# Projections and gates as high and low parts: gate chunks ahead of modulation chunks, x loaded first, attention's low parts on VectorE between the softmax steps

## The chip, the cores and the metric

One core of one Trainium2 chip. The metric is the device time of one launch in microseconds (us), lower is better. TensorE (PE), VectorE (DVE), ScalarE (ACT), GpSimd (POOL) and SyncE (SP, which issues the weight DMAs) each run a program of their own, in order, and meet at semaphores.

## The reference

Two layers of a four-branch mixer with an FFN over 256 tokens of width 1024, then a second block (a state-space scan, attention and experts), which the change doesn't touch. Of a layer:

```python
h = rms_norm(x, norm_mix_pre[l])
proj = h @ w_in[l]                                   # q, k, v, conv and pool inputs
... # compressed, selected, window and sink attention; conv; pooling
up = jnp.einsum("bsnc,ncd->bsnd", branches, w_branch[l])
gates = jax.nn.sigmoid((h @ w_gate[l]).reshape(bsz, seq, N_BRANCH, D_MODEL))
mix = jnp.einsum("bsnd,bsnd->bsd", gates, up) @ w_o[l]
x = x + rms_norm(mix, norm_mix_post[l])
hf = rms_norm(x, norm_ffn_pre[l])
u = causal_depthwise_conv(hf @ ffn_w_up[l], ffn_conv_w[l], ffn_conv_b[l])
gate, val = jnp.split(u, 2, axis=-1)
x = x + rms_norm((jax.nn.gelu(gate) * val) @ ffn_w_down[l], norm_ffn_post[l])
```

The second block also needs `silu(c) @ w_mod`, the modulation, which depends on no token.

## The kernel before

All matrices stream through one ring of four slots of 1 MB (128 x 2048 float32). SP reloads a slot when TensorE has given it back; a layer has 92 chunks, in the order in which TensorE takes them. TensorE gives a chunk back with the next product behind it (`release`, then `carry`), or with the chunk's own last one (`done_with`).

Products exist in two kinds. Plain float32 ones take a chunk straight from the ring: the projections kv, kv2, q and dq (L498, two chunks each, token-major, 512 columns), and the feature-major chunks c, ba, bg and gate (`blocks_fm`, L526, 16 products of 256 columns). The up, wo and FFN products use reduced-precision float32 (fp32r) three times in place of one: high x high, high x low and low x high. For these ACT rounds a chunk to its high part (`split_hi`, L386) and VectorE subtracts it from the chunk, which gives the low part (`split_lo`, L392).

The order of a layer is written out by hand for each engine. First four modulation chunks (`mods`, 0 and 1) run, then the transposition of the normed x (`ht`, L435), the projections, "ga" (the gates of the attention parts), c, ba, the compression (L555), bg. Then comes the attention loop. It has twelve items: for each half t of the queries three kinds of attention (selected, window, sink), each in two groups. An item has one block of 128 keys for t = 0 (the first six items) and two for t = 1. Pass i is, on TensorE: scores of item i (L640), a gate chunk, the transposition of item i-1's probabilities (`turn_probs`), its values (L666). On ACT: the gate's copy out, the copies of the transposed probabilities, the exponentials of item i. On VectorE: `mask(i)` (an add from PSUM, L1136, and a reduction, L1141 or L1144), `weigh(i-1)`, ten steps of the depthwise convolution (L1096). Two more gate chunks stand in passes 3 and 6, one in `cmp_out`, and behind the first eight gate chunks stands a modulation chunk each (`mod_half`, L448), with a turn (L467) every second time.

Behind the loop come the convolution's turn, the up products with the gates, wo, the residual and norm, the FFN.

Of the kernel before, what the change touches and what calls it, by code (L numbers as in the profile page):

```python
# [50 lines left out]
SPLITS = 3  # L51
FFN_CHUNKS = FB + FB // 2
# [5 lines left out]
def offsets(fields):  # L58
# [11 lines left out]
    ("w_ga", KD * 24),  # L70
])
ROWS, N_ROWS = offsets([("mix_post", D), ("ffn_post", D), ("sinks", 8)])
# [123 lines left out]
def plan_mods(jobs, steps):  # L196
    for i in steps:
        jobs.plan(("mod", i))
        if i - 1 in steps:
            jobs.plan(("modT", i - 1))  # L200


EARLY_MODS, MID_MODS = range(0, 2), range(2, MOD_STEPS)


def plan_layer(jobs):
    plan_mods(jobs, EARLY_MODS)
# [3 lines left out]
    jobs.plan(("modT", EARLY_MODS[-1]))  # L211
# [16 lines left out]
    for kv in range(2):  # L228
        jobs.plan(("hidT", kv), drains=2)
    jobs.plan(("bg", 1))  # L230
# [49 lines left out]
def layer_block(nc, l, mem, ring, landed, used, wts, psum, sems, cols_dram, rows_dram, loaded):  # L280
# [28 lines left out]
    lo_ready = sems("lo_ready")  # L309
# [9 lines left out]
    x, tm, hT, proj, gates, qTs, rkT = (mem[k] for k in ("x", "tm", "hT", "proj", "gates", "qTs", "rkT"))  # L319
# [3 lines left out]
    cdT = gates[:, 2048:3072].rearrange("p (m t) -> p m t", m=4)  # L323
    rtmp = gates[:, 3072:4480]
    rot = gates[:, 4480:7296].rearrange("p (t c) -> p t c", t=2)
    hfT, fT, split = (mem[k] for k in ("hfT", "fT", "split"))
# [9 lines left out]
    sg = sc[:, :, :, :].rearrange("p b j k -> p (b j k)")[:, 0:1024].rearrange("p (i c) -> p i c", i=2)  # L336
    pooled_in = mem["tmp"][:, :, :].rearrange("p i c -> p (i c)").rearrange("p (g t) -> p g t", g=4)
    small = mem["small"]
    mixT, bglu, cpad, acc, tmp, mixS, split2 = (mem[k] for k in ("hT", "bglu", "cpad", "acc", "tmp", "mixS", "split2"))
# [30 lines left out]
    n_up = 12  # L370
    first_ffn = N_LAYER_CHUNKS - 1 - FFN_CHUNKS
    first_up = first_ffn - n_up

    def split_slot(n):

        if n < n_up:
            return first_up + n, split2[:, n % 2, :, :], 2
        return first_ffn + n - n_up, split[:, (n - n_up) % SPLITS, :, :], SPLITS

    def split_hi(act, n):  # L380

        c, slot, turns = split_slot(n)
        if turns <= n < n_up or n >= n_up + turns:
            act.wait_ge(used[(c - turns) % SLOTS], l * (N_LAYER_CHUNKS // SLOTS) + ((c - turns) // SLOTS + 1))
# [3 lines left out]
    def split_lo(dve, n):  # L388

        c, slot, _ = split_slot(n)  # L390
        dve.wait_ge(hi_ready, n + 1)
        dve.tensor_tensor(slot[:, 1, :], ring[:, c % SLOTS, :], slot[:, 0, :].bitcast(F32), ALU.subtract).then_inc(lo_ready, 1)  # L392

    with nc.Block() as block:
# [11 lines left out]
        def _(pe):  # L406
# [49 lines left out]
            def mod(i):  # L456
                mod_half(i, 0)
                mod_half(i, 1)

            def mod_turn(i):  # L460

                jobs.wait_drained(pe, ("mod", i))
                if i == 0:
                    pe.wait_ge(loaded, 32)
# [8 lines left out]
            def mods(steps):  # L473
                for i in steps:
                    mod(i)
                    if i - 1 in steps:
                        mod_turn(i - 1)


            mods(EARLY_MODS)  # L480
            pe.wait_ge(loaded, 32)
# [4 lines left out]
            mod_turn(EARLY_MODS[-1])  # L486


            for w in ("kv", "kv2", "q", "dq"):
                for half in range(2):  # L490
                    chunk = next_chunk().rearrange("p (k n) -> p k n", k=4)
                    for t in range(TT):
                        if w == "kv":
                            jobs.wait_drained(pe, ("ht", half, t))
                        if half == 0:
                            jobs.claim(pe, (w, t))
                        for k in range(4):
                            mm = pe.matmul(jobs.out((w, t)), hT[:, 4 * half + k, t * P:(t + 1) * P], chunk[:, k, :],  # L498
                                           start=(half == 0 and k == 0), stop=(half == 1 and k == 3))
                            if k == 0:  # L500
                                carry(mm)
                        if half == 1 and t == 0:
# [9 lines left out]
            for t in range(TT):  # L512
                for k in range(KD):
                    mm = pe.matmul(jobs.out("ga")[:, 24 * t:24 * t + 24], hT[:, k, t * P:(t + 1) * P],
                                   C("w_ga", 24 * k, 24 * k + 24), start=(k == 0), stop=(k == KD - 1))
                    if k == 0:
                        carry(mm)
            jobs.fill(mm, "ga")

            def blocks_fm(name):  # L520

                chunk = next_chunk().rearrange("p (k m) -> p k m", k=KD)
                jobs.claim(pe, name)
                for b in range(2):
                    for k in range(KD):
                        mm = pe.matmul(jobs.out(name)[:, b * T:(b + 1) * T], chunk[:, k, b * P:(b + 1) * P], hT[:, k, :],  # L526
                                       start=(k == 0), stop=(k == KD - 1))
                        if k == 0:
                            carry(mm)
                jobs.fill(mm, name)  # L530
                return name

# [6 lines left out]
            for t in range(TT):  # L539
                jobs.wait_drained(pe, ("q", t))  # L540
                transpose4(("qT", t), [proj[:, t, 1024 + i * P:1024 + (i + 1) * P] for i in range(4)])
                pe.wait_ge(roped, 3 * t + 1)
# [21 lines left out]
            for kv in range(2):  # L564
# [7 lines left out]
                jobs.fill(mm, ("hidT", kv))  # L572
            release(blocks_fm(("bg", 1)))
# [15 lines left out]
            for t in range(TT):  # L589
                pe.wait_ge(roped, 3 * t + 2)  # L590
                transpose4(("rqT", t), [rot[:, t, 384 + i * P:384 + (i + 1) * P] for i in range(4)])
                pe.wait_ge(roped, 3 * t + 3)
# [96 lines left out]
            def next_split(n):  # L689

                c, slot, _ = split_slot(n)
                assert state["chunk"] == c, (state, c)
                state["chunk"] += 1
                pe.wait_ge(lo_ready, n + 1)
                return slot[:, 0, :], slot[:, 1, :]


            for bi, n in enumerate(BRANCH_ORDER):
                for half in range(2):
# [4 lines left out]
                    hi, lo = (part.rearrange("p (k n) -> p k n", k=4) for part in next_split(2 * bi + half))  # L704
# [20 lines left out]
            for c in range(2):  # L725
                for half in range(2):
                    hi, lo = (part.rearrange("p (k n) -> p k n", k=4) for part in next_split(8 + 2 * c + half))
# [24 lines left out]
            pe.wait_ge(h_lo, 2 * TT)  # L752
            for j in range(FB):
                hi, lo = (part.rearrange("p (k m) -> p k m", k=KD) for part in next_split(n_up + j))
# [14 lines left out]
            for i in range(FB // 2):  # L769
                hi, lo = (part.rearrange("p (k n) -> p k n", k=2) for part in next_split(n_up + FB + i))  # L770
# [20 lines left out]
            assert state["chunk"] == N_LAYER_CHUNKS, state  # L791
# [2057 lines left out]
```

## Time and profile before

| | |
|---|---|
| median of 3 runs | 2058.55 us (2053.18 to 2112.91) |
| the profiled execution's own time | 2053.64 us |
| its span | 2051.8 us |
| TensorE, VectorE, ACT, GpSimd busy | 91%, 46%, 32%, 11% |
| layer 0, layer 1, second block | about 0 to 645, 645 to 1265, 1265 to 2052 |

The profile shows one execution. A row of a timeline merges equal instructions that follow one another: it gives their start, the time they cover, their count and the idle time before them, with what ended it. A float32 product stands in it as two instructions. Where single products are listed, the difference of two starts is the pace, since the durations overlap.

### The profile page before, as it was taken

The numbers are of one execution on the slowest core, as the hardware profiler recorded it, in microseconds if no ns is written. First come the engines' busy times: TensorE is split into PE (matmuls) and PEld (weight loads), VectorE is DVE, ScalarE is ACT, GpSimd is POOL, SyncE is SP. The second block draws the span as 40 slices with busy tenths as digits, with TensorE's granted clock in tenths as the row PEclk, the third lists the DMA queues.
The fourth block names the chain that finished last, engine by engine and source line by source line (L and its number), as shares of the span: only waits on it lengthen the run. The fifth ranks groups of instructions, "written<-read, shape, count | busy, mean of one in ns | idle before, by whom it ended". The sixth has DMA issues, their size and how long they took to land. (4 is left out here: it accounts for less than half of the span.)

```text
span 2051.8 us, 24867 instructions
## 1 busy us (share of the span) xinstructions
PE 1860.6 (91%) x9940; PEld 1444.6 (70%) x9940; DVE 953.2 (46%) x1410; ACT 647.4 (32%) x987; POOL 217.5 (11%) x285
## 2 busy tenths in 40 slices
PE   6999998869996999998869997999899997899996
PEld 3577777869974477676859985544476645799995
DVE  1235464557742215454646743138434415355555
ACT  1122225445531112224545542111223401333331
POOL 0100000213310010000303320001520001000000
PEclk9999999989998999999989998899978997899998
DMA  7444422425455444522425545322110021355552
GB/s 275 143 185 164 185 84 102 152 106 182 180 182 219 163 184 145 204 85 80 154 97 182 185 168 188 123 82 82 41 42 1 1 103 62 106 183 189 179 183 82
DMA packets 39094, 279.81 MB, mean 136 GB/s; under 512 B 4432, under 2 KB 4688, under 8 KB 5840
## 3 DMA queue, kind: packets, MB, share of 16 engines
q1 hardware_dynamic: 37984, 272.44, 36.5%
q10 hardware_dynamic: 1008, 5.93, 0.8%
q8 instruction: 74, 1.21, 0.2%
q14 instruction: 28, 0.23, 0.0%
HBM read 277.30 MB, written 1.05 MB: 136 GB/s over the span
## 5 line engine op out<-in xcount | busy, mean ns | idle before, releaser
L526 PE MATMUL psum<-sb_hT,ring 128*128 128x256 f32 x1408 | 321.9, 388 | 2.2 <-DMA ring<-weights 2.1
L526 PEld LDWEIGHTS psum<-sb_hT,ring 128*128 128x128 f32 x1408 | 270.2, 194 | 49.1 <-issue 7.7
L392 DVE TENSOR_TENSOR sb_split<-ring,sb_split 128x2048 fp32r<-128x2048 f32 x90 | 212.4, 2360 | 123.7 <-ACT sb_split L386 123.4
L759 PE MATMUL psum<-sb_hfT,sb_split 128*128 128x256 f32 x704 | 201.4, 286 | 10.9 <-DVE sb_hfT L1279 10.9
L386 ACT ACTIVATE sb_split<-ring 128x2048 fp32r<-128x2048 f32 x90 | 171.9, 1910 | 114.9 <-PE psum L781 57.8
L762 PE MATMUL psum<-sb_hfT,sb_split 128*128 128x256 f32 x704 | 201.0, 286 | 0.0
L763 PE MATMUL psum<-sb_hfT,sb_split 128*128 128x256 f32 x704 | 200.9, 285 | 0.0
L1644 DVE TENSOR_TENSOR sb_split<-ring,sb_split 128x2048 fp32r<-128x2048 f32 x48 | 110.0, 2292 | 160.2 <-ACT sb_split L1639 160.2
L1937 PE MATMUL psum<-sb_hfS,sb_split 128*128 128x256 f32 x512 | 146.5, 286 | 2.5 <-PE psum L1959 2.1
L1940 PE MATMUL psum<-sb_hfS,sb_split 128*128 128x256 f32 x512 | 146.0, 285 | 0.0
L1941 PE MATMUL psum<-sb_hfS,sb_split 128*128 128x256 f32 x512 | 145.9, 285 | 0.0
L759 PEld LDWEIGHTS psum<-sb_hfT,sb_split 128*128 128x128 f32 x704 | 137.1, 195 | 11.4 <-DVE sb_hfT L1279 11.4
L762 PEld LDWEIGHTS psum<-sb_hfT,sb_split 128*128 128x128 f32 x704 | 137.1, 195 | 0.0
L763 PEld LDWEIGHTS psum<-sb_hfT,sb_split 128*128 128x128 f32 x704 | 137.0, 195 | 0.0
L1639 ACT ACTIVATE sb_split<-ring 128x2048 fp32r<-128x2048 f32 x48 | 91.6, 1908 | 95.8 <-PE psum L1898 47.0
L498 PE MATMUL psum<-ring,sb_hT 128*128 128x512 f32 x256 | 110.4, 593 | 0.0
L1937 PEld LDWEIGHTS psum<-sb_hfS,sb_split 128*128 128x128 f32 x512 | 99.4, 194 | 4.2 <-issue 3.8
L1309 DVE SCALAR_TENSOR_TENSOR sb_hq<-psum,sb_cols,sb_hq 128x254 f32<-128x254 f32 (+1 forms) x176 | 72.7, 475 | 61.8 <-ACT sb_hq L969 61.8
L1940 PEld LDWEIGHTS psum<-sb_hfS,sb_split 128*128 128x128 f32 x512 | 99.5, 194 | 0.3
L1941 PEld LDWEIGHTS psum<-sb_hfS,sb_split 128*128 128x128 f32 x512 | 99.4, 194 | 0.0
L1096 DVE SCALAR_TENSOR_TENSOR sb_acc<-sb_bglu,sb_cols,sb_acc 128x256 f32<-128x256 f32 x240 | 97.1, 476 | 0.0
L809 ACT ACTIVATE sb_gates<-psum 128x512 f32<-128x512 f32 x36 | 21.3, 597 | 232.7 <-PE psum L526 232.1
(352 smaller groups left out, 3221.2 us busy)
## 6 DMA issues: line engine op xcount, KB each, us to landing
ring<-weights SPq DMA_DIRECT2D x256, 1024.0 KB, 4.8
sb_rows<-rows ACTq DMA_DIRECT2D x2, 1028.0 KB, 10.6
sb_rows<-rows ACTq DMA_DIRECT2D x1, 2048.0 KB, 10.4
sb_cols<-cols ACTq DMA_DIRECT2D x2, 662.0 KB, 6.2
sb_x<-x_in SPq DMA_DIRECT2D x1, 1024.0 KB, 6.9
sb_y<-ctx_in SPq DMA_DIRECT2D x1, 1024.0 KB, 5.6
out<-sb_x SPq DMA_DIRECT2D x2, 512.0 KB, 2.7
sb_const<-const SPq DMA_DIRECT2D x1, 791.0 KB, 9.8
```

What stands on the lines that cost most here:

```text
L386: act.activation(slot[:, 0, :], ring[:, c % SLOTS, :], ACT.Copy).then_inc(hi_ready, 1)
L392: dve.tensor_tensor(slot[:, 1, :], ring[:, c % SLOTS, :], slot[:, 0, :].bitcast(F32), ALU.subtract).then_inc(lo_ready, 1)
L498: mm = pe.matmul(jobs.out((w, t)), hT[:, 4 * half + k, t * P:(t + 1) * P], chunk[:, k, :], start=(half == 0 and k == 0), stop=(half == 1 a ...
L526: mm = pe.matmul(jobs.out(name)[:, b * T:(b + 1) * T], chunk[:, k, b * P:(b + 1) * P], hT[:, k, :], start=(k == 0), stop=(k == KD - 1))
L759: mm = pe.matmul(out, hi[:, k, b * P:(b + 1) * P], hfT[:, 0, k, :], start=(k == 0), stop=False)
L762: pe.matmul(out, hi[:, k, b * P:(b + 1) * P], hfT[:, 1, k, :], start=False, stop=False)
L763: mm = pe.matmul(out, lo[:, k, b * P:(b + 1) * P], hfT[:, 0, k, :], start=False, stop=(k == KD - 1))
L1096: conv.up(dve.scalar_tensor_tensor(out=acc[:, b, :], in0=bglu[:, b, k:k + T], scalar=w, in1=acc[:, b, :], op0=ALU.mult, op1=ALU.add))
L1644: dve.tensor_tensor(split[:, n % SPLITS, 1, :], ring[:, (first_moe + n) % SLOTS, :], split[:, n % SPLITS, 0, :].bitcast(F32), ALU.subtract ...
L1937: mm = pe.matmul(out, hi[:, k, b * P:(b + 1) * P], hfS[:, 0, k, :], start=(k == 0), stop=False)
L1940: pe.matmul(out, hi[:, k, b * P:(b + 1) * P], hfS[:, 1, k, :], start=False, stop=False)
L1941: mm = pe.matmul(out, lo[:, k, b * P:(b + 1) * P], hfS[:, 0, k, :], start=False, stop=(k == KD - 1))
```

## The change

- c, ba, bg, gate and the four projections are done in three fp32r products. hS holds the high and low part of the normed, scaled x. High parts of chunks go to two shared buffers (hi; four in the FFN), low parts to a ring of their own, ring_low, with one slot per ring slot. In the attention loop VectorE takes the low part of gate chunk i+1 between `mask(i)` and `weigh(i-1)`, and ACT takes the high part of gate k+2 directly behind the copy of gate k.
- "ga" is computed with the weights held and 256 columns moving, and turned afterwards.
- The early modulation is gone: the six steps stand as twelve chunks behind gate chunks 0 to 11. Passes 3 and 6 have no second gate chunk; pass 12 has one. Gates are taken in the order of the branches.
- x and the constants are loaded ahead of the ring. The rows table is loaded behind the projections, its FFN part later still, into the same place.
- Buffers are laid out anew.

```diff
+def layer_chunks():
+    out = ["split"] * 12 + ["raw"] * 4 + ["split"] * 2
+    for i in range(16):
+        out.append("split")
+        if mid_mod_of(i) is not None:
+            out.append("raw")
+    return out + ["split"] * (12 + FFN_CHUNKS) + ["raw"]
...
+FIRST_C, FIRST_BA, FIRST_BG, FIRST_GATE, FIRST_UP, FIRST_WO, FIRST_FFN, FIRST_DOWN = 8, 10, 12, 14, 30, 38, 42, 64
...
     def split_hi(act, n):
+        before = n - HI_MIX if n <= FIRST_FFN else n - HI_FFN if n >= FIRST_FFN + HI_FFN - 1 else -1
+        if before >= 0:
+            c = SPLIT_CHUNKS[before]
+            act.wait_ge(used[c % SLOTS], l * (N_LAYER_CHUNKS // SLOTS) + (c // SLOTS + 1))
+        c = SPLIT_CHUNKS[n]
         act.wait_ge(landed[c % SLOTS], (l * (N_LAYER_CHUNKS // SLOTS) + (c // SLOTS + 1)) * 16)
-        act.activation(slot[:, 0, :], ring[:, c % SLOTS, :], ACT.Copy).then_inc(hi_ready, 1)
+        act.activation(hi_of(n), ring[:, c % SLOTS, :], ACT.Copy).then_inc(hi_ready, 1)
...
             def blocks_fm(name):
-                chunk = next_chunk().rearrange("p (k m) -> p k m", k=KD)
+                hi, lo = (part.rearrange("p (k m) -> p k m", k=KD) for part in next_split())
...
-                        mm = pe.matmul(jobs.out(name)[:, b * T:(b + 1) * T], chunk[:, k, b * P:(b + 1) * P], hT[:, k, :],
-                                       start=(k == 0), stop=(k == KD - 1))
+                        mm = pe.matmul(out, hi[:, k, bs], hS[:, 0, k, :], start=(k == 0), stop=False)
...
+                        pe.matmul(out, hi[:, k, bs], hS[:, 1, k, :], start=False, stop=False)
+                        mm = pe.matmul(out, lo[:, k, bs], hS[:, 0, k, :], start=False, stop=(k == KD - 1))
...
                     scores(i)
-                gate_chunks(i < len(ITEMS))
+                gate_chunks(1)
                 if i == 1:
                     cmp_out()
                 if i >= 1:
                     turn_probs(i - 1)
-                    gate_chunks(i in (3, 6))
                     values(i - 1)
...
                     i = gate_at["n"]
                     if i < 16:
-                        copy_out(("gate", i), gates[:, i * 512:(i + 1) * 512])
+                        n = BRANCH_ORDER[i // 4]
+                        copy_out(("gate", i), gate_of[n][:, i % 4 * 512:(i % 4 + 1) * 512], func=ACT.Sigmoid if n == BRANCH_ORDER[-1] and i > 13 else ACT.Copy)
+                        split_hi(act, FIRST_GATE + i + 2)
...
+            gate_lows = iter(range(FIRST_GATE, FIRST_GATE + 13))
+            split_lo(dve, next(gate_lows))
             for i in range(len(ITEMS) + 1):
                 if i < len(ITEMS):
                     mask(i)
+                    split_lo(dve, next(gate_lows))
...
+            split_lo(dve, FIRST_GATE + 13)
             out_low(len(ITEMS) - 1)
-            split_lo(dve, 0)
             conv_steps(4 * TAPS)
+            for n in range(FIRST_GATE + 14, FIRST_UP + 1):
+                split_lo(dve, n)
...
                     sp.dma_start(mem["cond"][:, :], cond).then_inc(conditioned, 16)
+                    sp.dma_start(mem["x"][:, :, :], x_in.rearrange("(t p) d -> p t d", p=P)).then_inc(loaded, 16)
+                    sp.dma_start(mem["const"][:, :], const).then_inc(placed, 16)
                     for s in range(SLOTS):
                         sp.dma_start(ring[:, s, :], weights[s]).then_inc(landed[s], 16)
```

ACT in the attention loop, one pass of before (pass 2): the gate's copy out, the modulation's, the transposed probabilities', the exponentials.

```order
L809 ACTIVATE sb_gates<-psum 128x512 [waits filled_a1]
L809 ACTIVATE sb_mrow<-psum 128x512 [waits filled_a3]
L809 ACTIVATE sb_pt<-psum 128x512 [waits filled_t]
L873 ACTIVATE sb_sc,sb_small<-sb_sc,sb_small 128x128 [waits masked]
L873 ACTIVATE sb_sc,sb_small<-sb_sc,sb_small 128x128 x3
```

The same place in the changed kernel. The chunk of the high part is in slot 0 (landed_0), and so was the gate chunk whose copy stands first; ISA is a wait for that slot's release.

```order
L822 ACTIVATE sb_tm<-psum 128x512 [waits filled_a2]
L403 ISA [waits used_0]
L404 ACTIVATE sb_hi<-ring 128x2048 [waits landed_0]
L822 ACTIVATE sb_mrow<-psum 128x512 [waits filled_a0]
L822 ACTIVATE sb_pt<-psum 128x512 [waits filled_t]
L906 ACTIVATE sb_sc,sb_small<-sb_sc,sb_small 128x128 [waits masked]
L906 ACTIVATE sb_sc,sb_small<-sb_sc,sb_small 128x128 x3
```

The high part has come between the gate's copy and the copy of the probabilities.

VectorE in the same loop, pass 3 of before: mask, weigh, convolution.

```order
L1136 TENSOR_TENSOR sb_sc<-psum,sb_const 128x4x128 [waits filled_s,filled_t]
L1141 TENSOR_REDUCE sb_small<-sb_sc 128x4 [waits drained_s]
L1164 RECIPROCAL sb_small<-sb_small 128x4 [waits exped]
L1167 TENSOR_TENSOR sb_small<-sb_small 128x4 [waits v_order]
L1170 TENSOR_TENSOR sb_sc<-sb_sc,sb_small 128x4x128 [waits v_order]
L1096 SCALAR_TENSOR_TENSOR sb_acc<-sb_bglu,sb_cols,sb_acc 128x256 [waits conv_done] x10
```

VectorE in pass 3 of the changed kernel (filled_s is the scores' signal).

```order
L1197 TENSOR_TENSOR sb_sc<-psum,sb_const 128x4x128 [waits filled_s,filled_t]
L1202 TENSOR_REDUCE sb_small<-sb_sc 128x4 [waits drained_s]
L410 TENSOR_TENSOR ring_low<-ring,sb_hi 128x2048 [waits hi_ready]
L1226 RECIPROCAL sb_small<-sb_small 128x4 [waits exped]
L1229 TENSOR_TENSOR sb_small<-sb_small 128x4 [waits v_order]
L1232 TENSOR_TENSOR sb_sc<-sb_sc,sb_small 128x4x128 [waits v_order]
L1157 SCALAR_TENSOR_TENSOR sb_acc<-sb_bglu,sb_cols,sb_acc 128x256 [waits conv_done] x10
```

The low part (L410) stands between the mask and weigh. TensorE of the changed kernel around it: the values of an item, the next item's scores, the next gate chunk, which waits for that low part (lo_dve).

```order
L690 MATMUL psum<-sb_pt,sb_proj 64x512 [waits drained_t]
L664 MATMUL psum<-sb_rkT,sb_qTs 128x128 [waits drained_s,drained_a1,drained_a2]
L664 MATMUL psum<-sb_rkT,sb_qTs 128x128 x3
L545 MATMUL psum<-sb_hS,sb_hi 128x256 [waits drained_a2,lo_dve]
L548 MATMUL psum<-sb_hS,sb_hi 128x256
```

Before, the gate chunk behind the scores waited for its chunk in the ring alone.

## Rows read from the trace of the kernel before

**Rows 1.** The page: busy time, share and instructions; TensorE and its clock by slice.
```profile
PE 1860.6 (91%) x9940; PEld 1444.6 (70%) x9940; DVE 953.2 (46%) x1410; ACT 647.4 (32%) x987; POOL 217.5 (11%) x285
...
PE   6999998869996999998869997999899997899996
...
PEclk9999999989998999999989998899978997899998
```
**Rows 2.** Timeline of TensorE: start us, us, engine, line, operation, count.
```profile
31.02 55.18 PE L498 MATMUL psum<-ring,sb_hT 128*128 128x512 f32 x128
86.03 3.65 PE L514 MATMUL psum<-sb_cols,sb_hT 128*128 128x24 f32 x32
...
163.88 7.17 PE L526 MATMUL psum<-sb_hT,ring 128*128 128x256 f32 x32
...
338.89 0.28 PE L717 MATMUL psum<-sb_brS,sb_split 128*128 128x256 f32 x1
339.01 0.28 PE L720 MATMUL psum<-sb_brS,sb_split 128*128 128x256 f32 x1
...
599.91 0.39 PE L777 MATMUL psum<-sb_split,sb_fT 128*128 128x512 f32 x1
600.14 0.39 PE L780 MATMUL psum<-sb_split,sb_fT 128*128 128x512 f32 x1
```
**Rows 3.** The same view: start, two passes and end of layer 0's attention loop.
```profile
151.79 1.16 PE L640 MATMUL psum<-sb_rkT,sb_qTs 64*128 64x128 f32 x8
...
185.78 7.17 PE L526 MATMUL psum<-sb_hT,ring 128*128 128x256 f32 x32
...
195.24 1.07 PE L666 MATMUL psum<-sb_pt,sb_proj 128*64 128x512 f32 x2 [0.70 <-ACT sb_pt L809]
...
281.94 0.66 PE L435 MATMUL psum<-sb_const,sb_sc 128*128 128x128 f32 x4 [0.74 <-ACT sb_pt L809]
282.53 1.93 PE L666 MATMUL psum<-sb_pt,sb_proj 128*64 128x512 f32 x4
284.39 1.99 PE L640 MATMUL psum<-sb_rkT,sb_qTs 64*128 64x256 f32 x8
...
337.66 1.04 PE L435 MATMUL psum<-sb_const,sb_acc 128*128 128x128 f32 x8
```
**Rows 4.** By line: high and low parts, duration in ns (min/median/max).
```profile
L386 ACT ACTIVATE sb_split<-ring x90: 1892/1908/1921, 331.2 to 1245.1; 128x2048 fp32r<-128x2048 f32 x90
...
L392 DVE TENSOR_TENSOR sb_split<-ring,sb_split x90: 2282/2293/2929, 333.2 to 1247.0; 128x2048 fp32r<-128x2048 f32 x90
```
**Rows 5.** The chunk's successor on TensorE, SP's reload, and 160 to 330's reloads until landed.
```profile
161.80 1.06 PE L448 MATMUL psum<-ring,sb_cvec 128*32 128x512 f32 x8
...
163.03 2.06 SPq L402 DMA_DIRECT2D ring<-weights  x2
...
DMA to landing us min/median/max: 4.7/4.9/8.0
```
**Rows 6.** By line: the mask's add and reduction, ns (min/median/max).
```profile
L1136 DVE TENSOR_TENSOR sb_sc<-psum,sb_const x12: 682/958/1225, 155.3 to 312.0; 128x512 f32<-128x512 f32 x6, 128x1024 f32<-128x1024 f32 x6
...
L1141 DVE TENSOR_REDUCE sb_small<-sb_sc x8: 686/954/1220, 156.0 to 287.8; 128x4 f32<-128x512 f32 x4, 128x4 f32<-128x1024 f32 x4
```
**Rows 7.** Timeline of TensorE around the wait for the ring, and the bg chunk behind.
```profile
125.42 1.68 PE L555 MATMUL psum<-ring,sb_gates 128*32 128x256 f32 x16 [2.94 <-DMA ring<-weights]
127.90 9.46 PE L526 MATMUL psum<-sb_hT,ring 128*128 128x256 f32 x32 [0.81 <-DMA ring<-weights]
```
**Rows 8.** Windows: stretch, length, TensorE busy (instructions), granted clock, DMA share, GB/s.
```profile
396.00:397.00 1.00, 1.00 (x3) 0.50 0.95 131
...
399.00:400.00 1.00, 1.00 (x6) 1.00 0.26 107
```
**Rows 9.** Timeline of VectorE: the norm's scaling, layer 0 and layer 1.
```profile
18.82 1.42 DVE L992 TENSOR_SCALAR sb_tm<-sb_x,sb_small 128x1024 f32<-128x1024 f32 x2 [18.82 <-DMA sb_rows<-rows]
...
653.30 1.42 DVE L992 TENSOR_SCALAR sb_tm<-sb_x,sb_small 128x1024 f32<-128x1024 f32 x2 [13.24 <-DMA sb_rows<-rows]
```

More of the change, by code:

```diff
@@ L511, in _ @@
             jobs.claim(pe, "ga")
-            for t in range(TT):
+            for part in range(2):
                 for k in range(KD):
-                    mm = pe.matmul(jobs.out("ga")[:, 24 * t:24 * t + 24], hT[:, k, t * P:(t + 1) * P],
-                                   C("w_ga", 24 * k, 24 * k + 24), start=(k == 0), stop=(k == KD - 1))
-                    if k == 0:
+                    mm = pe.matmul(jobs.out("ga")[32 * (k % 4):32 * (k % 4) + 32, 0:T], C("w_ga", 32 * k, 32 * k + 32),
+                                   hS[:, part, k, :].bitcast(F32), start=(part == 0 and k < 4), stop=(part == 1 and k >= 4))
+                    if part == 0 and k == 0:
                         carry(mm)
@@ L572, in _ @@
                 jobs.fill(mm, ("hidT", kv))
+            jobs.wait_drained(pe, "ga")
+            jobs.claim(pe, "gaT")
+            for t in range(TT):
+                mm = pe.matmul(jobs.out("gaT")[:, 24 * t:24 * t + 24], gaT[:, t * P:(t + 1) * P], K("sel", 0, 24), start=True, stop=True)
+            jobs.fill(mm, "gaT")
             release(blocks_fm(("bg", 1)))
@@ L703, in _ @@
                             transpose4(("obT", t), [ln_tm[:, t, b * P:(b + 1) * P] for b in range(4)])
-                    hi, lo = (part.rearrange("p (k n) -> p k n", k=4) for part in next_split(2 * bi + half))
+                    hi, lo = (part.rearrange("p (k n) -> p k n", k=4) for part in next_split())
                     if half == 0:
@@ L726, in _ @@
                 for half in range(2):
-                    hi, lo = (part.rearrange("p (k n) -> p k n", k=4) for part in next_split(8 + 2 * c + half))
+                    hi, lo = (part.rearrange("p (k n) -> p k n", k=4) for part in next_split())
                     for i in range(2):
@@ L840, in _ @@
                     copy_out(("hidT", kv), dst, src, func=ACT.Gelu_apprx_tanh)
-            for i in range(2):
-                copy_out(("bg", i), sg[:, i, :], func=ACT.Sigmoid)
+            split_hi(act, FIRST_GATE)
+            copy_out(("bg", 0), sg[:, 0, :], func=ACT.Sigmoid)
+            copy_out("gaT", small[:, 0:48], jobs.out("gaT")[:, 0:48], func=ACT.Sigmoid)
+            copy_out(("bg", 1), sg[:, 1, :], func=ACT.Sigmoid)
+            split_hi(act, FIRST_GATE + 1)
             for t in range(TT):
@@ L934, in _ @@
                 act.activation(mixS[:, 0, 2 * i:2 * i + 2, :], mixT[:, 2 * i:2 * i + 2, :], ACT.Copy).then_inc(mix_hi, 1)
-            for n in range(9, n_up):
+            for n in range(FIRST_WO + 1, FIRST_FFN):
                 split_hi(act, n)
@@ L1231, in _ @@
                     jobs.wait_filled(dve, name)
-                    g2 = gates[:, n * 2048 + i * 512:n * 2048 + (i + 1) * 512]
+                    g2 = gate_of[n][:, i * 512:(i + 1) * 512]
+                    if n == BRANCH_ORDER[-1] and i >= 2:
+                        jobs.wait_drained(dve, ("gate", 12 + i))
                     if bi == 0:
@@ L1254, in _, with residual @@
                                   ALU.subtract).then_inc(mix_lo, 1)
-            for n in range(9, n_up):
+            for n in range(FIRST_WO + 1, FIRST_FFN + 1):
                 split_lo(dve, n)
-            def residual(kind, g, first):
+            def residual(kind, first):
                 for t in range(TT):
@@ L2652, in place @@
                     mem1[k] = stack.enter_context(nc.sbuf_tensor(f"sb_{k}", [P, *s], dtype))
+            place(first, MEM_HI)
             with ExitStack() as phase:
@@ L2656, in build_program @@
             place(first, MEM_BR1)
+            with ExitStack() as phase:
+                place(phase, MEM_ROT)
             with ExitStack() as phase:
@@ L2661, in build_program @@
                 place(phase, MEM_UP)
-            for fields, dtype in ((MEM_FFN_SPLIT, F32R), (MEM_FFN, F32)):
-                for k, s in fields.items():
-                    mem1[k] = first.enter_context(nc.sbuf_tensor(f"sb_{k}", [P, *s], dtype))
+            place(first, MEM_FFN)
             with nc.Block() as block:
@@ L2700, in build_program @@
             with nc.Fori(0, LAYERS) as l:
-                layer_block(nc, l, mem1, ring, landed, used, weights, psum, sems, cols, rows, loaded)
+                layer_block(nc, l, mem1, ring, ring_low, landed, used, weights, psum, sems, cols, rows, loaded, placed)
                 nums = [s.num for s in layer_sems]
@@ L2754, in gates_and_mods @@
     for n in range(16):
-        out.append(gate[n:n + 1])
+        at = 4 * BRANCH_ORDER[n // 4] + n % 4
+        out.append(gate[at:at + 1])
         step = mid_mod_of(n)
```

349 lines of the change are left out of this document (186 added, 163 removed).

## The prediction, made before the changed kernel ran

> **What bounds the kernel now.** I read the page first. TensorE is busy in 91% of the span, and the slices show it at 9 tenths nearly everywhere, the attention part included, at the full granted clock [rows 1]. So a stage is worth what TensorE spends in it, and the first question is what the new products cost there. The timeline of TensorE gives that [rows 2]. A float32 chunk of a projection takes 55.18 / 8 = 6.90 us, and a gate chunk 7.17 us (16 products of 256 columns, 0.45 us each). In the stages that already work with two parts, the reduced products of 256 columns start 0.12 us apart, those of 512 columns 0.23 us apart (the durations printed there overlap, so their starts count). The second question is who TensorE waits for in the attention loop, because ACT and VectorE get new work there. Now they barely hold it: the loop runs from 151.79 to 338.45, 186.7 us, and its usual wait is 0.7 us for ACT's copy of the transposed probabilities [rows 3].
>
> **Products.** Three reduced products replace one float32 product. A gate chunk becomes 48 x 0.12 = 5.76 us, 1.41 less. A projection chunk becomes 24 x 0.227 = 5.45, 1.45 less. There are 22 feature-major chunks a layer (6 in front of the attention loop, 16 gates) and 8 projection chunks. "ga" falls from 3.65 us to an estimated 2.2: 16 products, four abreast, of 256 columns, and two short ones.
>
> The Trainium skill (FP8 and Floating Point Precision, "TensorE Precision Notes") says that a true float32 product takes four passes. By that rule three passes would save a quarter, 1.79 us of 7.17 in place of 1.41, and some 17 us more over 44 chunks. The rows differ, since 0.12 us is more than a quarter of 0.45, and I keep theirs.
>
> **Split work.** Each of these 30 chunks now needs 1.91 us of ACT for the high part and 2.29 us of VectorE for the low part [rows 4], and waits for both. In the projections this fits: with two high buffers, chunk n is released when n-2 ends, and 4.2 us of splitting lie beside the 5.45 us of chunk n-1. VectorE's rotations fit between. So the 8 chunks gain 11.6 us, the six others 8.5, "ga" 1.4. The last of the six (bg) give back about 3.8, because their high part can start only when a chunk in a slot just released has landed (TensorE waits for that ring already [rows 7], and now splitting follows behind it), and about 2.0 are lost where the copy of the turned queries stands behind the high part of gate chunk 1. Net some -15 per layer, -30 in all.
>
> **The attention loop, ACT.** Here the order decides. A gate chunk and a modulation chunk alternate, so gate k+2 is four chunks behind gate k: the same ring slot. ACT copies gate k out and then at once takes the high part of gate k+2, which waits for the slot to be reloaded. Behind that wait, in order, stand the copy of the transposed probabilities (TensorE waits for it), the exponentials and, later, VectorE. Let E be the end of a gate chunk. The slot is released by the first modulation product: the chunk ended at 161.8 and the reload was issued at 163.03, E+1.2. A reload lands after a median of 4.9 us [rows 5], at E+6.1. The high part ends at E+8.0, the copy at E+8.6. Now it ends at about E+2.3: chunk end 192.95, values product at 195.24 [rows 3]. The new wait holds for k = 0 to 10; behind it the modulation chunks run out and the chunk is there.
>
> **The attention loop, VectorE.** In pass i (from 2 on) TensorE does scores(i) and then gate i+1, whose low part VectorE takes only after mask(i), and mask(i) needs scores(i). So TensorE stands still from the end of the scores for an add and a reduction, 0.7 us each in the first six items and 1.2 each in the last six [rows 6], and 2.3 us for the low part. Nothing hides it: the next instruction of TensorE is the waiting one.
>
> A period of the first kind is then 8.6 + 1.1 values + 1.2 scores + 1.4 mask + 2.3 low part + 5.8 gate + 0.4 for handovers = 20.8 us (my estimate for a handover is 0.1). One of the second kind has another transposition (0.7), values 1.9, scores 2.0, mask 2.4: 24.2 us. Over the loop: 33.2 to the end of the third gate chunk (in this stretch the copies of the compressed attention wait for one reload); four periods of 20.8 and 1.1 for the sink operations; a mixed one of 22.7; four of 24.2; 19.9 for the first without reload wait; 16.6 and 21.2 for the last three chunks, where low parts queue behind weigh(11) and out_low(11); 1.0 for the turn of the convolution. Sum 295.7 against 186.7: +109.0 per layer, +218. The modulation chunks moved in (4 x 1.06 and two turns) are in it, since they lie under the reload wait.
>
> **The clock.** After idle gaps of 2 to 3 us rows show half the granted clock: behind the ring wait at 122.5 to 125.4 a chunk took 9.46 us in place of 7.17 [rows 2, 7], and in the up products the clock stood at 0.50 at 396, back at 1.00 at 399 [rows 8]. Each period now has two gaps, of about 5 and 4 us, with 2 to 5 us of work between. At the low level the work between them costs about 2 us more and the start of the gate chunk again about 2 (2.3 in the row). I take 4.0 for each of ten periods: 40 per layer, 80 in all. The bounds are nothing, and 5.5 in 12 periods (132).
>
> The Trainium skill (TensorE: Matmul & The Clock Gate, "HAM oscillation") tells of a kernel whose bursts start cold every time because it waits between them. That speaks against this change, and the trace agrees in the places named: by that rule the 80 is due, without it the sum ends at 2233.
>
> **Starts of the layers.** In layer 0 the first scaled tile is held at 18.8 us by the rows table [rows 9], and projections start at 31.0. Now x comes first, the rows table is needed much later, and the early modulation is gone. Squares, root, norm, turn, scaling, high and low parts and the first chunk's low part, added up from the arrival of x at an estimated 7 us, end at about 19.2; with 2 us for a cold start, 10 us are won. In layer 1 the norm no longer waits (653.3 becomes about 650.6), but scaling, high and low parts take the 2.7 us back, and TensorE starts cold: +1. Together -9. Elsewhere I count nothing: the later stages have one more high buffer and TensorE has them full already.
>
> **Sum.** 2053.6 (the profiled execution's own time, 1.8 over its span; the median of the runs shown is 2058.55, 0.2% more) + 218 + 80 - 30 - 9 = 2312.6, say 2312 us.
>
> **Rivals.** First, the other side: all splitting stays under TensorE and only its count matters. Then 44 x 1.41 + 16 x 1.45 + 2 x 1.4 + 9 = 97.0 are won: 1957 us. For it speak shares of 46% for VectorE and 32% for ACT [rows 1], against it the order. It is one mechanism with a clear point: it holds if each high part finds its chunk landed and each low part is done when the scores are. Chance 0.04.
>
> Second, the reload is not waited for, only VectorE is: then a period is 5.3 us shorter (8.0 becomes 2.7), ten of them 53 per layer, and one gap is left for the clock (40 in all): 2053.6 + 112 + 40 - 39 = 2167. It would need the reload under way much sooner than [rows 5] have it. Chance 0.10.
>
> Third, both waits come but the clock holds: 2233. That lies inside the forecast's range.
>
> Forecast, both waits: 0.86. The range goes from 2200 (no clock cost, and 15% off the added loop time) to 2390 (5.5 for the clock in 12 periods, and 25 for queues behind queues that I did not follow). A measurement of this kernel tells about 2% from no change. Faster by over 2%: 0.04; within 2%: 0.01; slower: 0.95.
>
> **What would show it.** In the new profile: reduced gate products 0.12 us apart in a warm chunk; ACT's high parts idle for the DMA of the ring, about 4.5 us each, some 20 of them; the copies of the probabilities 5 us later than the transpositions; TensorE's gate chunks idle for VectorE's low part, 3.7 to 4.7 us each, some 20; the clock near 0.5 around them; gate chunks 20 to 29 us apart. The forecast is wrong if the loop takes under 250 us a layer, if the high parts wait for TensorE and not for the DMA, or if TensorE stays at 9 tenths there.

## The result, and the profile after

The changed kernel takes **2348.69 us** (median of four runs, 2347.57 to 2351.46) against 2059.22 us before (four runs, 2053.18 to 2112.91). One of the four runs before, 2112.91 us, fell in a slower state that some executions of any kernel show; the ratio leaves it out. The ratio is **1.142**, 95% interval 1.139 to 1.145: slower by 14%. The profiled execution took 2347.57 us, its span 2345.8.

The page after, the parts that answer to [rows 1], and then some of its costliest groups (busy us, mean ns | idle before, releaser):

```profile
PE 1884.6 (80%) x10780; PEld 1519.5 (65%) x10780; DVE 1085.0 (46%) x1478; ACT 754.8 (32%) x1055; POOL 261.6 (11%) x285
PE   7875565696999597565568799879998999799996
PEclk9987667797999797776779889989998799789998
...
L410 DVE TENSOR_TENSOR ring_low<-ring,sb_hi 128x2048 fp32r<-128x2048 f32 x118 | 270.9, 2297 | 238.3 <-ACT sb_hi L404 238.3
L404 ACT ACTIVATE sb_hi<-ring 128x2048 fp32r<-128x2048 f32 x118 | 225.7, 1913 | 400.8 <-DMA ring<-weights 249.2
L545 PE MATMUL psum<-sb_hS,sb_hi 128*128 128x256 f32 x704 | 232.2, 330 | 134.7 <-DVE ring_low L410 127.0
...
L690 PE MATMUL psum<-sb_pt,sb_proj 128*64 128x512 f32 x72 | 63.5, 1018 | 78.8 <-ACT sb_pt L822 78.8
```

Read it from the slices: TensorE is at 5 and 6 tenths in slices 4 to 8 and again in 17 to 21, which lie in the two attention loops, and its clock falls with it. ACT and VectorE are no busier than their 32% and 46%, so no engine has become the bound. The groups say who waits for whom: TensorE for VectorE's low part (127.0 us) and for ACT's copy of the probabilities (78.8), ACT for the reload of the ring (249.2).

One pass of the loop on TensorE, from the end of one gate chunk to the end of the next (timeline: start us, us, engine, line, operation, count, idle before):

```profile
222.23 1.06 PE L467 MATMUL psum<-ring,sb_cvec 128*32 128x512 f32 x8
...
224.14 0.64 PE L454 MATMUL psum<-sb_const,sb_sc 128*128 128x128 f32 x4
230.75 1.97 PE L690 MATMUL psum<-sb_pt,sb_proj 128*64 128x512 f32 x2 [5.97 <-ACT sb_pt L822]
232.65 2.07 PE L664 MATMUL psum<-sb_rkT,sb_qTs 64*128 64x128 f32 x8
239.09 0.58 PE L545 MATMUL psum<-sb_hS,sb_hi 128*128 128x256 f32 x1 [4.37 <-DVE ring_low L410]
```

And the same pass on ACT and then on VectorE:

```profile
222.33 0.60 ACT L822 ACTIVATE sb_gates<-psum 128x512 f32<-128x512 f32 x1 [13.79 <-PE psum L549]
228.30 1.91 ACT L404 ACTIVATE sb_hi<-ring 128x2048 fp32r<-128x2048 f32 x1 [5.37 <-DMA ring<-weights]
230.12 0.58 ACT L822 ACTIVATE sb_pt<-psum 128x512 f32<-128x512 f32 x1
...
246.44 0.60 ACT L822 ACTIVATE sb_gates<-psum 128x512 f32<-128x512 f32 x1 [14.21 <-PE psum L549]
```

```profile
234.83 0.69 DVE L1197 TENSOR_TENSOR sb_sc<-psum,sb_const 128x512 f32<-128x512 f32 x1 [10.13 <-PE psum L664]
235.55 0.69 DVE L1206 TENSOR_REDUCE sb_small<-sb_sc 128x4 f32<-128x512 f32 x1
...
236.75 2.29 DVE L410 TENSOR_TENSOR ring_low<-ring,sb_hi 128x2048 fp32r<-128x2048 f32 x1
```

ACT stands at the high part until the ring is reloaded (228.30), and the copy that TensorE wants is one instruction behind it (230.12). VectorE stands at the mask until TensorE's scores are there (234.83), and the low part that TensorE wants comes behind the mask (236.75). The two waits are 5.97 and 4.37 us, and the pass takes 246.44 - 222.33 = 24.1 us.

### The profile page after: what moved, and what is told of

Its sections match the earlier page's. It is cut to its first block and busy times, and to the rows that moved or that the text cites. A ratio compares the mean times of both kernels' runs of the same rounds, so it can differ in the third digit from the quotient of the medians.

```text
span 2345.8 us, 26767 instructions
## 1 busy us (share of the span) xinstructions
PE 1884.6 (80%) x10780; PEld 1519.5 (65%) x10780; DVE 1085.0 (46%) x1478; ACT 754.8 (32%) x1055; POOL 261.6 (11%) x285
## 5 line engine op out<-in xcount | busy, mean ns | idle before, releaser
L410 DVE TENSOR_TENSOR ring_low<-ring,sb_hi 128x2048 fp32r<-128x2048 f32 x118 | 270.9, 2297 | 238.3 <-ACT sb_hi L404 238.3
L404 ACT ACTIVATE sb_hi<-ring 128x2048 fp32r<-128x2048 f32 x118 | 225.7, 1913 | 400.8 <-DMA ring<-weights 249.2
L545 PE MATMUL psum<-sb_hS,sb_hi 128*128 128x256 f32 x704 | 232.2, 330 | 134.7 <-DVE ring_low L410 127.0
L545 PEld LDWEIGHTS psum<-sb_hS,sb_hi 128*128 128x128 f32 x704 | 162.8, 231 | 152.1 <-DVE ring_low L410 143.5
L548 PE MATMUL psum<-sb_hS,sb_hi 128*128 128x256 f32 x704 | 224.9, 319 | 0.0
L549 PE MATMUL psum<-sb_hS,ring_low 128*128 128x256 f32 x704 | 223.0, 317 | 0.0
L777 PE MATMUL psum<-sb_hfT,ring_low 128*128 128x256 f32 x704 | 197.8, 281 | 0.0
L1704 DVE TENSOR_TENSOR sb_split<-ring,sb_split 128x2048 fp32r<-128x2048 f32 x48 | 110.0, 2292 | 159.9 <-ACT sb_split L1699 159.9
L548 PEld LDWEIGHTS psum<-sb_hS,sb_hi 128*128 128x128 f32 x704 | 162.9, 231 | 0.0
L549 PEld LDWEIGHTS psum<-sb_hS,ring_low 128*128 128x128 f32 x704 | 162.0, 230 | 0.0
L690 PE MATMUL psum<-sb_pt,sb_proj 128*64 128x512 f32 x72 | 63.5, 1018 | 78.8 <-ACT sb_pt L822 78.8
L1699 ACT ACTIVATE sb_split<-ring 128x2048 fp32r<-128x2048 f32 x48 | 91.6, 1908 | 95.5 <-PE psum L1958 47.0
L773 PE MATMUL psum<-sb_hfT,sb_hi 128*128 128x256 f32 x352 | 100.7, 286 | 10.4 <-DVE sb_hfT L1046 10.4
L410 DVE TENSOR_TENSOR ring_low<-ring,sb_hi_ffn 128x2048 fp32r<-128x2048 f32 x32 | 73.3, 2292 | 72.0 <-ACT sb_hi_ffn L404 72.0
L776 PE MATMUL psum<-sb_hfT,sb_hi 128*128 128x256 f32 x352 | 100.0, 284 | 0.0
```

The source lines that it names most:

```text
L404: act.activation(hi_of(n), ring[:, c % SLOTS, :], ACT.Copy).then_inc(hi_ready, 1)
L410: eng.tensor_tensor(low_of(n), ring[:, SPLIT_CHUNKS[n] % SLOTS, :], hi_of(n).bitcast(F32), ALU.subtract)\
L545: mm = pe.matmul(out, hi[:, k, bs], hS[:, 0, k, :], start=(k == 0), stop=False)
L548: pe.matmul(out, hi[:, k, bs], hS[:, 1, k, :], start=False, stop=False)
L549: mm = pe.matmul(out, lo[:, k, bs], hS[:, 0, k, :], start=False, stop=(k == KD - 1))
L773: mm = pe.matmul(out, hi[:, k, b * P:(b + 1) * P], hfT[:, 0, k, :], start=(k == 0), stop=False)
```

## The experiments

The time after, 2348.69 us, is what "less" and "more" refer to.

The theory is that the two waits, and with them nearly all of the loss, come of the order of instructions on ACT and on VectorE. The rival is that splitting is too much work for the two.

**The high part out of the way (`e1_hi_late`).** In the loop ACT takes the high part behind the exponentials, not behind the copy of the gate chunk.

```diff
+            held = []
...
-                        split_hi(act, FIRST_GATE + i + 2)
+                        if hold:
+                            held.append(FIRST_GATE + i + 2)
+                        else:
+                            split_hi(act, FIRST_GATE + i + 2)
...
-                    gate_out(1)
+                    gate_out(1, True)
...
                 if i < len(ITEMS):
                     exps(i)
+                while held:
+                    split_hi(act, held.pop(0))
```

> In the attention loop ACT takes the high parts of gate chunks behind the exponentials of the pass; VectorE's order stays. Theory (both waits bind): the wait for the copy of the probabilities (6.0 to 7.3 us each) goes, the wait for the low part behind the scores (3.8 to 4.9 us) stays; 20 waits of 5.3 us are 106 us, with up to 2 us of clock each 146: 2200 to 2245 us. Rival A (only VectorE's place costs, ACT's wait lies beside it): no change, 2340 to 2350. Rival B (ACT's place is the whole loss): back to about 2060.

Measured 2177.07 us (ratio to before 1.058, 1.054 to 1.063): 171.6 less, more than expected. One wait went that isn't among the twenty: in pass 1 TensorE waited 7.46 us (layer 0) for ACT's copy of the compressed attention, and now waits 0.74. The same pass now (timeline of TensorE):

```profile
201.94 1.07 PE L467 MATMUL psum<-ring,sb_cvec 128*32 128x512 f32 x8
...
205.17 1.07 PE L690 MATMUL psum<-sb_pt,sb_proj 128*64 128x512 f32 x2 [0.69 <-ACT sb_pt L822]
206.17 1.16 PE L664 MATMUL psum<-sb_rkT,sb_qTs 64*128 64x128 f32 x8
211.69 0.58 PE L545 MATMUL psum<-sb_hS,sb_hi 128*128 128x256 f32 x1 [4.36 <-DVE ring_low L410]
...
219.65 1.07 PE L467 MATMUL psum<-ring,sb_cvec 128*32 128x512 f32 x8
```

The pass is 17.7 us (201.94 to 219.65), 6.4 less: 5.3 from the wait (5.97 to 0.69), and 1.8 from the values and scores, which last 1.07 and 1.16 us where they lasted 1.97 and 2.07; the gate chunk gives 0.7 back (7.96 us, before 7.24). The wait for ACT had cost its own length and also the clock of what came behind. The low part's wait stands unchanged at 4.36.

**The low part ahead of the mask (`e2_lo_first`).**

```diff
                 if i < len(ITEMS):
+                    split_lo(dve, next(gate_lows))
                     mask(i)
-                    split_lo(dve, next(gate_lows))
```

> VectorE takes a gate chunk's low part ahead of the mask of the pass, not behind it; ACT's order stays. Theory: the wait behind the scores goes (20 of 3.8 to 4.9 us, 86 in all) and the gate chunk starts some 1.7 us sooner to run warm where the clock comes back: 2230 to 2265 us. ACT's wait stays at 6 to 7 us. Rival B (only ACT's place costs): under 10 us, 2340. Rival A: about 2060.

Measured 2239.67 us (1.089, 1.084 to 1.093): 109.0 less, inside what was expected. The wait for the low part is gone: the gate chunk (227.62) follows the scores at once, and the pass is 20.3 us (215.09 to 235.39). The wait for the probabilities stays, and all behind it runs cold, the gate chunk at 7.77 us too:

```profile
215.09 1.07 PE L467 MATMUL psum<-ring,sb_cvec 128*32 128x512 f32 x8
...
223.72 1.97 PE L690 MATMUL psum<-sb_pt,sb_proj 128*64 128x512 f32 x2 [6.08 <-ACT sb_pt L822]
225.62 2.07 PE L664 MATMUL psum<-sb_rkT,sb_qTs 64*128 64x128 f32 x8
227.62 0.58 PE L545 MATMUL psum<-sb_hS,sb_hi 128*128 128x256 f32 x1
...
235.39 1.07 PE L467 MATMUL psum<-ring,sb_cvec 128*32 128x512 f32 x8
```

**Both (`e3_both`).** The two edits together.

> Both orders changed together. Theory: no long wait is left in the loop, TensorE is the bound there again and at full clock; the loop takes 175 to 185 us a layer in place of 341, in all 2015 to 2045 us, below the kernel before (2059), since the cheaper products then show. Rival C (the loop is long for another reason, more products or DMA of the modulation chunks): over 2150.

Measured 2052.68 us (eight runs, 0.998, 0.997 to 1.000): 296.0 less, where the two gains alone add up to 280.6. So both waits cost by order: the split work is all still there, and the kernel is back at the time of before. It is 8 us above what was expected: a loop takes 193.7 us, not 175 to 185, since waits for the low part are left in front of gate chunks 0, 3, 13 and 14 (4.05, 3.36, 4.75 and 4.03 us in layer 0). The pass shown above now takes 11.2 us on TensorE (195.56 to 206.73):

```profile
195.56 1.07 PE L467 MATMUL psum<-ring,sb_cvec 128*32 128x512 f32 x8
...
198.79 1.07 PE L690 MATMUL psum<-sb_pt,sb_proj 128*64 128x512 f32 x2 [0.69 <-ACT sb_pt L822]
199.80 1.16 PE L664 MATMUL psum<-sb_rkT,sb_qTs 64*128 64x128 f32 x8
200.88 0.39 PE L545 MATMUL psum<-sb_hS,sb_hi 128*128 128x256 f32 x1
...
206.73 1.07 PE L467 MATMUL psum<-ring,sb_cvec 128*32 128x512 f32 x8
```

The gate chunk takes 5.85 us here (200.88 to 206.73), 7.24 in the changed kernel (239.09 to 246.33), 7.96 in `e1_hi_late` (211.69 to 219.65) and 7.77 in `e2_lo_first`: with either wait left it starts at half the clock. So the second edit takes 3.8 us from this pass when made alone (24.1 to 20.3) and 6.5 once the first is made (17.7 to 11.2). In the later passes the two differ less; over the whole kernel it is 109.0 and 124.4 us.

**The clock by itself (`e5_fill`).** The two waits are filled with throwaway products (36 in front of the values of items 0 to 9, 24 in front of the gate chunk of passes 2 to 11; they go into the region that the next gate chunk clears), so that TensorE is kept busy while the waits themselves stay.

```diff
+            def idle_work(n):
...
+                        pe.matmul(jobs.out(name)[:, 0:T], hS[:, 0, i % KD, 0:P], hS[:, 0, i % KD, :], start=True, stop=True)
...
+                if 2 <= i < len(ITEMS):
+                    idle_work(24)
                 gate_chunks(1)
...
+                    if i < 11:
+                        idle_work(36)
                     values(i - 1)
```

> The changed kernel with throwaway products (into the next gate chunk's own bank, which its first product clears) in both waits of the attention loop: 36 of 256 columns ahead of the values, 24 ahead of the gate chunk, passes 2 to 11. At full clock they take 4.3 and 2.9 us, less than the waits of 6.0 to 7.4 and 3.8 to 4.9. The waits stay, only TensorE's idleness goes. Theory (half the granted clock behind the waits costs some 3.4 us per pass: values 1.97 for 1.07, scores 2.07 for 1.16, gate chunk 7.42 for 5.76): values, scores and chunk are back at 1.07, 1.16 and 5.8, and 55 to 70 us go: 2280 to 2295 us. Rival (the slow products have another cause, and filling only adds work): 2350 to 2400.

Measured 2327.83 us (1.131, 1.129 to 1.134): 20.9 less, well short of what was expected, though the mean granted clock rose from 0.862 to 0.906. TensorE's timeline, two passes of layer 0, one behind the other:

```profile
203.33 1.07 PE L697 MATMUL psum<-sb_pt,sb_proj 128*64 128x512 f32 x2 [3.02 <-ACT sb_pt L833]
204.34 2.03 PE L671 MATMUL psum<-sb_rkT,sb_qTs 64*128 64x128 f32 x8
206.29 5.31 PE L642 MATMUL psum<-sb_hS 128*128 128x256 f32 x24
...
217.21 1.07 PE L467 MATMUL psum<-ring,sb_cvec 128*32 128x512 f32 x8
...
225.70 1.07 PE L697 MATMUL psum<-sb_pt,sb_proj 128*64 128x512 f32 x2 [1.64 <-ACT sb_pt L833]
226.71 1.16 PE L671 MATMUL psum<-sb_rkT,sb_qTs 64*128 64x128 f32 x8
232.22 0.38 PE L545 MATMUL psum<-sb_hS,sb_hi 128*128 128x256 f32 x1 [1.30 <-DVE ring_low L410]
238.07 1.06 PE L467 MATMUL psum<-ring,sb_cvec 128*32 128x512 f32 x8
```

Where 1.64 us were left of the wait, values, scores and gate chunk ran at full clock (1.07, 1.16, 5.85) and the pass took 20.9 us (217.21 to 238.07) instead of 24.1. Where 3.02 were left, the scores were cold again (2.03), and the cold filler behind them (L642) took 5.31 us, longer than the wait of 3.77 that it fills; that pass took 22.9 us instead of 24.1.

The shortfall is not there, though. Count the passes from the end of one gate chunk to the end of the next, as above. In the six that hold the values of items 0 to 5, the gain is 20.7 us in layer 0 (153.0 to 132.3) and 20.9 in layer 1: 3.5 a pass, as the theory has it. The next four hold the values of items 6 to 9, which have two blocks of keys. There the wait for ACT's copy comes in front of the second block's transposition, inside `turn_probs`, and the filler stands behind it:

```profile
346.64 1.11 PE L454 MATMUL psum<-sb_const,sb_sc 128*128 128x128 f32 x4 [7.32 <-ACT sb_pt L833]
347.41 6.21 PE L642 MATMUL psum<-sb_hS 128*128 128x256 f32 x36
```

It fills nothing and adds some 6 us of work, so these four passes take 11.8 us longer in layer 0 (108.8 to 120.5). So the run bears out the price per pass in the first six, and its total does not measure the clock's whole share.

**The bank behind the last two chunks (`e4_gat`).** In front of the loop, ahead of the second bg chunk, TensorE waits for ACT's copy of the first (3.88 us), a wait that I had not counted. The changed kernel, timeline of TensorE:

```profile
108.74 0.58 PE L545 MATMUL psum<-sb_hS,sb_hi 128*128 128x256 f32 x1 [5.17 <-DVE ring_low L410]
...
116.18 0.97 PE L587 MATMUL psum<-sb_const,sb_pt 128*128 128x30 f32 x8
...
121.47 0.55 PE L545 MATMUL psum<-sb_hS,sb_hi 128*128 128x256 f32 x1 [3.88 <-ACT sb_sc L822]
...
129.40 0.42 PE L604 MATMUL psum<-sb_hidk,sb_cols 128*64 128x15 f32 x8
```

and ACT beside it:

```profile
117.51 1.91 ACT L404 ACTIVATE sb_hi<-ring 128x2048 fp32r<-128x2048 f32 x1
119.44 1.28 ACT L822 ACT_TABLE_LOAD   x1
120.73 0.60 ACT L822 ACTIVATE sb_sc<-psum 128x512 f32<-128x512 f32 x1
```

"gaT" is a new entry in the rotation over four PSUM banks, and it moves the second bg chunk into the bank of the first, whose copy (120.73) stands behind a high part and a table load. `e4_gat` takes "gaT" out of the rotation:

```diff
-    jobs.plan("gaT")
+    jobs.plan("gaT", "t")
```

> The changed kernel, but the turned ga (gaT) takes a PSUM bank outside the rotation of four, so that the second bg chunk's bank is no longer the one of the first bg chunk. Theory: its wait for ACT's copy of bg 0 (3.9 us a layer) and the half clock behind it (2.3) go: 8 to 13 us, 2336 to 2341 us. Rival (the chunk would wait as long for its parts): no change, 2347 to 2350.

Measured 2337.94 us (1.137, 1.133 to 1.141): 10.7 less, as expected. The wait of 3.88 is gone, and the loop of layer 0 starts at 130.12 us, not at 136.72.

**x behind the first chunk (`e8_x_late`).** How much of the early start is due to x being loaded first?

```diff
-                    sp.dma_start(mem["x"][:, :, :], x_in.rearrange("(t p) d -> p t d", p=P)).then_inc(loaded, 16)
-                    sp.dma_start(mem["const"][:, :], const).then_inc(placed, 16)
                     for s in range(SLOTS):
                         sp.dma_start(ring[:, s, :], weights[s]).then_inc(landed[s], 16)
+                        if s == 0:
+                            sp.dma_start(mem["x"][:, :, :], x_in.rearrange("(t p) d -> p t d", p=P)).then_inc(loaded, 16)
+                            sp.dma_start(mem["const"][:, :], const).then_inc(placed, 16)
```

> The changed kernel with the first ring chunk loaded ahead of x and the constants, as before the change. Theory: x and the constants come 1 MB later, 2.4 us, and the first projection starts at about 22.4 in place of 19.96 us; the rest of the 11.1 us by which it starts earlier than before the change stays, since it is due to the rows table and the early modulation. Rival (x first is most of it): it starts at 26 us or later.

Measured 2346.47 us, a single run, 2.2 below the median after. The total does not resolve it; the timeline does. The first projection starts at 22.14 us in this kernel (first row), at 19.96 in the changed one (second row):

```profile
22.14 0.79 PE L516 MATMUL psum<-sb_hi,sb_hS 128*128 128x512 f32 x1 [4.46 <-DVE ring_low L410]
```

```profile
19.96 0.80 PE L516 MATMUL psum<-sb_hi,sb_hS 128*128 128x512 f32 x1 [5.38 <-DVE ring_low L410]
```

The 2.2 us were as forecast. They are a fifth of the 11.1 us won at the start; the later rows table and the early modulation, which left the path, were not tried apart. What became of the 2.2 us in the rest of the run stays open: the second block starts 1.0 later and the span ends 1.1 earlier.

**A version that beats both (`e6_best`).** `e3_both` and `e4_gat`, and VectorE takes the low part of gate 0 ahead of the convolution's steps, those of gates 13 and 14 ahead of and behind the last weighing, since `e3_both` still waited 4.05 us for the first and 4.75 for the second.

```diff
+            split_lo(dve, FIRST_GATE)
             conv_at = {"n": 0}
...
+                if i == len(ITEMS):
+                    split_lo(dve, FIRST_GATE + 13)
                 if i >= 1:
                     weigh(i - 1)
+                if i == len(ITEMS):
+                    split_lo(dve, FIRST_GATE + 14)
```

> Both orders changed as in the run before, gaT outside the rotation, the low part of gate 0 taken ahead of the convolution's first steps, those of gates 13 and 14 ahead of and behind weigh(11). Theory: the waits of 4.05, 4.75 and 4.03 us in front of gates 0, 13 and 14 go, and the 3.9 us of bg 1, each with some half clock behind it: 30 to 45 us below 2052.7, 2008 to 2022 us, below the kernel before. Rival (other waits take their places): above 2040.

Measured **2007.82 us** (ratio 0.975, 0.974 to 0.977), 2.5% faster than before and at the lower edge of what was expected. Its page, answering to [rows 1]:

```profile
PE 1787.0 (89%) x10780; PEld 1451.7 (72%) x10780; DVE 1084.3 (54%) x1478; ACT 757.1 (38%) x1055; POOL 261.7 (13%) x285
```

The instructions are the same in number as in the changed kernel, and ACT and VectorE work as long as there (757.1 and 754.8, 1084.3 and 1085.0 us). Only their order and the bank of "gaT" differ, and the time by 340.9 us. The rival "too much work" is out.

**The first bg chunk between the halves of the compression (`e7_bg`).** `e6_best` still waits 5.68 us for the low part of that chunk. Here the chunk's place in the order changes, and "gaT" is back in the rotation.

```diff
-    out = ["split"] * 12 + ["raw"] * 4 + ["split"] * 2
+    out = ["split"] * 12 + (["raw"] * 2 + ["split"]) * 2
...
+    jobs.plan(("hid", 0))
     jobs.plan(("bg", 0))
+    jobs.plan(("hid", 1))
```

> As e6, but gaT inside the rotation again and the first bg chunk between the two halves of the compression, so that its slot comes free two chunks sooner. Theory: TensorE's wait for bg 0's low part (5.7 us, with 2.7 us of half clock) and the wait of 2.9 us for the ring go or shrink: 8 to 20 us below e6. Rival (the wait moves to the second half of the compression or to bg 1): the same as e6 within 4 us.

Measured 2006.18 us (0.975, 0.973 to 0.977), the same as `e6_best`. The wait went elsewhere (timeline of TensorE):

```profile
110.97 1.25 PE L588 MATMUL psum<-sb_const,sb_pt 128*128 128x30 f32 x8 [1.69 <-ACT sb_pt L823]
116.96 1.02 PE L596 MATMUL psum<-sb_const,sb_pt 128*128 128x24 f32 x4 [4.74 <-ACT sb_sc L823]
```

1.69 and 4.74 us for ACT's copies, which stand behind high parts (and the second behind a table load of 1.28 us as well).

## Why the prediction was right, and where its terms were off

The forecast was 2312 us with 2200 to 2390, slower. Measured: 2348.69. In the profiles, the parts as the prediction cut them (layer 0, layer 1), each the difference of two starts on TensorE:

| part | predicted | measured |
|---|---|---|
| start to the first projection | -10 | -11.1 |
| projections to the loop | -15, -15 | -4.0, -2.7 |
| the loop, with the clock | +149, +149 | +154.7, +155.1 |
| behind the loop of layer 0, up to the down products | 0 | -2.0 |
| start of layer 1 | +1 | +3.4 |
| behind the loop of layer 1, up to the second block | 0 | -0.3 |
| sum | +259 | +293.1 |

**Right: both waits and their cause.** ACT's high part idles for the reload (11 times in the loop of either layer, 57.6 and 58.1 us, 5.3 each; the chunk that ended at 222.23 was followed by a landed reload at 228.30, 6.1 us later, as put). The copy of the probabilities comes behind it, and the low part comes behind a mask that waits for the scores. The pass was put at 20.8 and 4.0 for the clock, 24.8; it takes 24.1. `e1_hi_late` and `e2_lo_first` take the two waits out one at a time, and `e3_both` takes out 296.0 us, as much as the whole loss.

**Right: the clock inside the passes.** The step said 4.0 us for each of ten passes. In the pass shown, measured against `e3_both` from start to start, the values lose 0.90, the scores 0.98 and the gate chunk 1.39: 3.3 us, and the pass of `e5_fill` is 3.2 shorter. That is one of the cheapest. Over the nine passes from 198.09 to 436.00 us of layer 0, with all idle time taken off, TensorE's work lasts 37.5 us longer than the same work in `e3_both`: 3.2 to 5.3 us a pass, 4.2 in the mean. The Trainium skill (TensorE: Matmul & The Clock Gate, "HAM oscillation") was cited for bursts that start cold after each wait; by that rule the products behind both waits had to be slow, and the rows show it (values 1.97 and 1.07, scores 2.07 and 1.16). The rival "both waits, but the clock holds" (2233) falls.

**Short by 5.7 and 6.1: the ends of the loop.** Against the terms of the sum, layer 0: up to the end of the third gate chunk 37.5 us for 33.2; the nine passes behind it 237.9 for 239.8 (36 for the clock in it); the rest 65.9 for 62.7. So the passes came out as put, and the surplus lies at the two ends, where the sum had nothing for the clock: gate chunks 0 and 2 take 8.0 and 7.5 us, not 5.85, and the values of the last two items 3.3 and 3.5 us, where `e3_both` has 1.93.

**Wrong: "Net some -15 per layer".** This is the term that was furthest off, by 23 us of the 34 that are missing. Split by starts in layer 0 ([rows 2, 3, 7] and after):

- The eight projections: -8.5 (55.0 to 46.5), put at -11.6. Eight products at the beginning start 0.43 apart, at half clock (the 2 us that I had booked at the start), and the warm ones 0.233, not 0.227.
- "ga" and the next four chunks with their rotations: -3.8, put at -7.1. Two chunks take 11.38 us against 13.82, 1.22 saved in each and not 1.41, because my 7.17 was a duration that overlaps the next start; and between the pairs TensorE waits 1.49 us for a copy by ACT and 0.67 behind "ga".
- The ring wait and the first bg chunk: +2.3, put at +2.4. Right.
- From there to the loop: +6.0, put at +0.6. Here is the wait for the bank, 3.88 us, with a cold second bg chunk behind it (121.47 to 129.40, 7.9 us). `e4_gat` shows it: 10.7 us for the two layers. I had read the new entry "gaT" for its products and not for its place in the rotation. The 2.0 booked for the copy of the turned queries were too much: TensorE waits 0.36 us there (at 133.09).

**Other rivals.** "All splitting stays under TensorE", 1957 us, described what the change could do and not what its order does: `e6_best` comes within 51 us of it. "The reload is not waited for", 2167, is what `e1_hi_late` builds: 2177.07. Its reading of that one wait was good, the condition was not met.

## What to carry to other kernels

Work that is light by its share can still be dear by its place: on an engine that works in order, an instruction that waits for a reload or for another engine makes everything behind it wait. Before such work goes into a busy loop, look at what is next in that queue and put it behind the last instruction for which the bottleneck waits; 296 us lay in that choice here. A new entry in a rotation of buffers moves every later one: write out which buffer each of the next takes, and whose copy it then waits for. Between a pair of waits count the clock too: 3.2 to 5.3 us a pass here, on top of 8 to 12 us of idle.

## What the runs showed of the hardware

- **Filler that left about 3 us idle did not keep everything behind it warm.** In the first six filled passes of `e5_fill`, layer 0, the products behind were all warm where 1.64 and 1.75 us had been left idle in front of the values. Where 3.02, 3.08 and 3.10 had been left, something ran slow each time, but not the same thing: the scores (2.03 for 1.16) and the next filler (5.31 for 3.13), the same two by less (1.49 and 4.30), the gate chunk alone (7.38 for 5.85). I had expected filler to hold the clock in every pass.
- **The clock's price falls behind the wait that lowers it.** The windows of the changed kernel in this pass (stretch, length, TensorE busy, granted clock, DMA share, GB/s):

```profile
228.00:229.00 1.00, 0.00 (x0) 0.77 0.95 401
...
241.00:242.00 1.00, 1.00 (x6) 0.50 0.00 0
243.00:244.00 1.00, 1.00 (x10) 1.00 0.00 0
```

The clock is falling while TensorE still stands idle (0.77 at 228), it is 0.50 (1.2 of 2.4 GHz) well into the gate chunk that began at 239.09, and full at 243, while that chunk is still running. So the price is paid by products behind the wait.
- **Each edit alone gains less than behind the other.** 171.6 and 109.0 us for either edit, 296.0 for both. Read from the other side, over `e3_both`, ACT's wait alone costs 187.0 us (`e2_lo_first`) and VectorE's alone 124.4 (`e1_hi_late`), 311.4 in sum, more than the 296.0 of the two together: in the passes with the values of items 0 to 5, either wait alone is enough to make the gate chunk behind it start cold.
